# A two-block model on one core: the gates' product in column groups, the decay rows as split halves, SiLU moved to the second job

## The chip, the cores and the metric

The kernel runs on one core of a Trainium2 chip. The time is the device time of one execution in microseconds (us). Five engines work side by side and meet at semaphores: PE (TensorE, matrix products), DVE (VectorE), ACT (ScalarE), POOL (GpSimd) and SP (SyncE, which issues most DMAs).

## The reference

Two blocks run one after the other over 256 positions of width 1024. The change lies in the first layer of the first block, a gated delta rule with 8 heads, cut here to what matters:

```python
qkv = jax.nn.silu(causal_conv(proj[..., :3072], w_conv))        # q, k, v
a = proj[..., 4096:4104]; b = proj[..., 4104:4112]              # 16 more columns: the gates
g = -jnp.exp(a_log) * jax.nn.softplus(a + dt_bias)              # 8 heads x 256 positions
beta = jax.nn.sigmoid(b)
g = jnp.cumsum(g, axis=-1)                                      # within a chunk
decay = jnp.exp(jnp.where(tril, g[..., :, None] - g[..., None, :], -jnp.inf))
a_mat = jnp.where(strict, einsum(k * beta, k) * decay, 0.0)     # solved against
```

Behind it come the rest of this layer, an attention layer, and a second block whose conditioning vector also passes a SiLU (`cond = silu(c)`). These are not touched but for the place of that one SiLU and of one Square.

## The kernel before

**Jobs.** All large projections are cut into 104 jobs of 256 output columns. A chunk of weights (1 MB) comes by DMA into one of three slots `raw`. ACT rounds each half of it into `whi` (helper `high`, L1013), DVE subtracts to get the remainder `wlo` (helper `low`, L1444), and PE multiplies three times per tile (`whi` by `hhi`, `whi` by `hlo`, `wlo` by `hhi`; all at L489, 48 products a job, 8 tiles k of 6 products). Products of these split halves (type fp32r in the profile) stand in for one exact float32 product. Job J accumulates in bank `ps0` or `ps1` in turn.

**Jobs 0 to 7** make keys and queries, two heads a job. Each is followed by a convolution of four taps: the first tap on ACT (`first_tap`, L1092), three on DVE (`conv(J)`, L1511, 6 instructions), then SiLU on ACT (`silu(J)`, L1097). After an odd job PE sums the squares of the keys (`key_sums`), which waits for a Square of ACT (L1102). The loop of DVE is, for each J, `low(J + 1)` and then `conv(J)`; that of ACT is `high(J + 1)`, `silu(J - 1)`, `first_tap(J)`. The order on each engine is the order in which the code is written.

**The gates.** Behind job 0 PE multiplies the 16 gate columns (`w_ab`, held in the arena) by the unsplit activations `hf_a` in 8 float32 products that accumulate in `ps3[0:16]`, then one small product for attention biases (`onehot`). DVE makes the gate rows `rt16` from it behind `conv(0)` (L1560, L1562), ACT takes their Exp and Ln in job 1, DVE scans them behind `conv(2)` into `r16` (row h: summed log decay of head h).

**The delta rule.** Behind job 7, `decay_rows(p)` spreads the rows of two heads over 128 partitions: for each head one float32 product of `r16[:, 0, :]` (16 partitions x 256) by a column of the identity. ACT reads the bank (`state_decay`, L1141), PE adds the causal mask (`masked(p)`), ACT takes the Exp (`decay`, L1150), DVE multiplies (`pair_matrices`). Pieces of job 8 (`parts(8, ...)`) stand between. Then triangular inverses are built level by level (`lv` 1 to 6), each level with a job (9 + lv) beside it. Job 11 writes over the bank that `conv(9)` reads, so PE waits for `conv(9)` before it; on DVE this stands behind the scaling of keys (L1652), `low(11)` and `take_rows(1)` (L1629).

**POOL** sets constants at the start and, once `conv(0)` is done, builds masks and identity copies, last a copy of 128x2048 numbers (L426). PE starts when six of the first memsets are counted (`ones_ok`).

## Time and profile before

| | us |
|---|---|
| median of 3 runs | 833.12 (832.19 to 843.05) |
| the profiled execution, its own time | 833.37 |
| span of its profile | 831.5 |
| PE busy | 814.4 (98%) |
| DVE busy | 603.0 (73%) |
| ACT busy | 486.6 (59%) |
| POOL busy | 43.6 (5%) |

The profiled execution took 1.9 us more than its span, and 0.25 us more than the median. A row of the timeline gives the start, the time, engine and line, what is written and read, the number of instructions merged into it, and in brackets how long the engine had been idle and what released it. A float32 product is recorded as two instructions. Ends of products are modelled and overlap; the distance of their starts is the better measure.

### The profile page before, as it was taken

The page shows a single profiled execution, that of the slowest core. Times are in us where ns is not written, and L with a number is a line of the kernel's source. Part 1 is how long each engine was busy: PE and PEld are TensorE (multiplying, and loading weights), DVE is VectorE, ACT ScalarE, POOL GpSimd, SP SyncE. Part 2 cuts the span into 40 slices and gives each one's busy share as a digit, 9 for nine tenths or more (in the row PEclk, how much of TensorE's full clock was granted, in tenths as well). Part 3 has the DMA queues.
Part 4 walks back from the last instruction along what each step waited for, and adds up shares of the span by engine and source line. Part 5 has one row for each costly group of instructions (what it writes and reads, how often), then busy time and mean ns, then how long its engine had stood idle before and what let it go on. Part 6 is the DMA issues. An engine that isn't in the chain of part 4 may idle for free.

```text
span 831.5 us, 17292 instructions
## 1 busy us (share of the span) xinstructions
PE 814.4 (98%) x7278; PEld 793.7 (95%) x7278; DVE 603.0 (73%) x1049; ACT 486.6 (59%) x761; POOL 43.6 (5%) x68
## 2 busy tenths in 40 slices
PE   8999999999999999999999999989999999999998
PEld 7899999989999999999999999989999999999998
DVE  4776976678887876878797985556777867565662
ACT  5756756646855466553535354347777767677731
POOL 0500000018000100000000001000000000000000
PEclk9999999999999999999999999999999999999999
DMA  7363234526866884386666664973555644443450
GB/s 289 113 240 110 103 108 149 148 82 218 252 227 236 224 328 153 109 296 208 248 208 248 222 236 127 247 232 107 203 199 203 207 149 153 152 166 140 152 178 26
DMA packets 26493, 153.78 MB, mean 185 GB/s; under 512 B 2848, under 2 KB 3376, under 8 KB 12080
## 3 DMA queue, kind: packets, MB, share of 16 engines
q1 hardware_dynamic: 24432, 146.37, 50.3%
q0 software_dynamic: 1984, 6.31, 4.0%
q8 instruction: 58, 0.95, 0.5%
q14 instruction: 19, 0.16, 0.1%
HBM read 150.04 MB, written 2.62 MB: 184 GB/s over the span
## 4 chain that ended last, share of the span: by engine, by line
PE 84%; DVE 7%; DMA 4%; ACT 3%; issue 1%; SPq 0%; DVEq 0%; ACTq 0%
PE ps L489 83%; DMA raw<-weights 4%; DVE wlo L1444 3%; ACT whi L1013 1%; PE ps L869 1%; DVE early L1629 0%; DVE hlo L1472 0%; DVE arena L1476 0%; DVE early L1511 0%; DVE arena L1511 0%; DVE arena L1652 0%; DVE ada_ring L1525 0%; DVE olo L1489 0%; ACT hhi L1043 0%; PE ps L738 0%
## 5 line engine op out<-in xcount | busy, mean ns | idle before, releaser
L1444 DVE TENSOR_TENSOR wlo<-raw,whi 128x1024 fp32r<-128x1024 f32 x224 | 267.7, 1232 | 113.8 <-ACT whi L1013 113.8
L489 PE MATMUL ps<-hhi,whi 128*128 128x256 f32 x1024 | 295.0, 288 | 5.3 <-DVE hlo L1472 1.7
L489 PE MATMUL ps<-hlo,whi 128*128 128x256 f32 x1024 | 290.2, 283 | 0.0
L489 PE MATMUL ps<-hhi,wlo 128*128 128x256 f32 x1024 | 290.1, 283 | 0.0
L1013 ACT ACTIVATE whi<-raw 128x1024 fp32r<-128x1024 f32 x224 | 227.1, 1054 | 88.2 <-PE ps L489 60.9
L489 PEld LDWEIGHTS ps<-hhi,whi 128*128 128x128 f32 x1024 | 196.5, 192 | 8.2 <-issue 5.3
L489 PEld LDWEIGHTS ps<-hlo,whi 128*128 128x128 f32 x1024 | 196.7, 192 | 0.4
L489 PEld LDWEIGHTS ps<-hhi,wlo 128*128 128x128 f32 x1024 | 196.6, 192 | 0.0
L489 PE MATMUL ps<-ohi,whi 128*128 128x256 f32 x448 | 128.8, 287 | 1.4 <-DVE olo L1489 1.3
L489 PE MATMUL ps<-olo,whi 128*128 128x256 f32 x448 | 126.7, 283 | 0.0
L489 PE MATMUL ps<-ohi,wlo 128*128 128x256 f32 x448 | 126.7, 283 | 0.0
L489 PEld LDWEIGHTS ps<-ohi,whi 128*128 128x128 f32 x448 | 85.9, 192 | 2.8 <-issue 2.1
L489 PEld LDWEIGHTS ps<-olo,whi 128*128 128x128 f32 x448 | 85.9, 192 | 0.5 <-issue 0.5
L489 PEld LDWEIGHTS ps<-ohi,wlo 128*128 128x128 f32 x448 | 85.9, 192 | 0.0
L489 PE MATMUL ps<-arena 128*128 128x256 f32 (+2 forms) x496 | 76.5, 303 | 1.1 <-DVE olo L1489 1.1
L489 PEld LDWEIGHTS ps<-arena 128*128 128x128 f32 (+1 forms) x496 | 69.0, 187 | 7.4 <-issue 3.2
L489 PE MATMUL ps<-whi,hhi 128*128 128x256 f32 x256 | 72.6, 284 | 0.0
L489 PE MATMUL ps<-whi,hlo 128*128 128x256 f32 x256 | 72.4, 283 | 0.0
L489 PE MATMUL ps<-wlo,hhi 128*128 128x256 f32 x256 | 72.4, 283 | 0.0
L1525 DVE SCALAR_TENSOR_TENSOR ada_ring<-ada_ring,sil 128x256 f32<-128x256 f32 x144 | 59.0, 478 | 0.0
L489 PEld LDWEIGHTS ps<-whi,hhi 128*128 128x128 f32 x256 | 49.0, 192 | 0.7 <-issue 0.4
L489 PEld LDWEIGHTS ps<-whi,hlo 128*128 128x128 f32 x256 | 49.1, 192 | 0.3
(232 smaller groups left out, 961.4 us busy)
## 6 DMA issues: line engine op xcount, KB each, us to landing
raw<-weights SPq DMA_DIRECT2D x112, 1024.0 KB, 5.0
ada_ring<-ada SPq DMA_DIRECT2D x24, 1024.0 KB, 5.1
arena<-bias_rows_d POOLq DMA_DIRECT2D x4, 512.0 KB, 15.8
x<-x_t SPq DMA_DIRECT2D x2, 512.0 KB, 4.7
arena<-bias_rows_b POOLq DMA_DIRECT2D x4, 256.0 KB, 7.8
bias_rows_d<-turns POOLq DMA_DIRECT2D x1, 1024.0 KB, 13.3
arena<-bias_rows_d POOLq DMA_DIRECT2D x4, 256.0 KB, 19.5
out_t<-x SPq DMA_DIRECT2D x4, 256.0 KB, 2.4
```

The lines of the kernel that those rows point to most:

```text
L489: return pe.matmul(o, l, r, start=start, stop=stop, skip_group_check=skip)
L869: m = pe.transpose(turned_bank(hh, soft0)[:, a * P:a * P + P], ts[:, hh, c0:c0 + P], ident)
L1013: act.activation(whi[:, unit % UNITS, :, :], raw[:, c % RAW, 4 * half:4 * half + 4, :], ACT.Copy).then_inc(hi_ok_sem, 1)
L1444: dve.tensor_tensor(wlo[:, unit % UNITS, :, :], raw[:, c % RAW, 4 * half:4 * half + 4, :], whi[:, unit % UNITS, :, :].bitcast(F32), ALU.su ...
L1525: own(dve.scalar_tensor_tensor(out=b, in0=b, scalar=sil[:, k:k + 1], in1=ring[:, :, k - 2, :], op0=ALU.mult, op1=ALU.add))
```

## The change

Three things are changed.

1. *The gates' product.* The 8 products of the gate columns go to four groups of 32 output partitions of `ps6`, group k mod 4, two to a group. The first four read 32 columns, of which the upper 16 belong to the next tile and are ignored later. DVE copies the bank to `ab_quarters` (in the arena) ahead of `conv(0)`. In the midst of job 1, at tile 4, PE adds up the four groups with one float32 product by `ab_join`, a matrix of zeros and ones that DVE reduces from the identity. The gate rows are then made in turn J = 1, ahead of `conv(1)`.
2. *The decay rows.* Behind `conv(3)` DVE rounds `r16[:, 0, :]` into `r48[0:16]` (fp32r) and subtracts to get `rlo`; a DMA on POOL's queue moves `rlo` to `r48[32:48]`; the rest of `r48` is set to zero by a seventh memset at the start. `decay_rows` multiplies `r48` (48 partitions) by a column of `pick48`, which has a one at h and at 32 + h: one fp32r product a head instead of one float32 product.
3. *SiLU.* The Square of `final_norm` and the SiLU of `cond`, both 128x8, leave ACT's stretch between the activations' split and `high(1)`, and stand behind `first_tap(1)`. The SiLU's table load moves with it, to the front of `silu(0)`.

```diff
@@ pool
             pool.memset(rt16[:, 3, :], 1.0).then_inc(ones_ok_sem, 1)
+            pool.memset(r48[:, :].bitcast(F32), 0.0).then_inc(ones_ok_sem, 1)
             pool.wait_ge(conv_ok_sem, 1)
...
+            pool.wait_ge(rows_lo_sem, 1)
+            pool.dma_start(r48[32:48, :], rlo[:, :]).then_inc(rows_up_sem, 16)
             pool.wait_ge(bias_sb_sem, 1)
@@ tensor
+            def ab_rows():
+
+                pe.wait_ge(ab_copy_sem, 2)
+                mm(ps[3][0:16, 0:S], ab_join[:, :], ab_quarters, True, True).then_inc(ab_ok_sem, 1)
...
                     for k in range(KT):
-                        m = mm(ps[3][0:16, 0:S], A(6144, 8, 16)[:, k, :], hf_a[:, k, :], k == 0, k == KT - 1)
-                    m.then_inc(ab_ok_sem, 1)
+                        g, rows = k % 4, 32 if k < 4 else 16
+                        m = mm(ps[6][32 * g:32 * g + rows, 0:S], A(6144 + 16 * k, rows), hf_a[:, k, :], k < 4, True)
+                    m.then_inc(ab_quarter_sem, 1)
...
-                job(2 * i + 1, "T", hhi, hlo)
+                job(2 * i + 1, "T", hhi, hlo, at={4: ab_rows} if i == 0 else {})
...
-                    m = mm(ps[2 + 3 * (p % 2)][:, hh * S:hh * S + S], ident[0:16, h:h + 1].to_broadcast([16, P]), r16[:, 0, :], hh == 0, False)
+                    m = mm(ps[2 + 3 * (p % 2)][:, hh * S:hh * S + S], pick48[:, h:h + 1].to_broadcast([48, P]), r48[:, :], hh == 0, False)
...
+            pe.wait_ge(rows_up_sem, 16)
+            pe.wait_ge(rows_lo_sem, 2)
             decay_rows(0)
@@ scalar
             split_h(0, hf_a, hhi)
-            act.activation(gq, cols[:, COLS["final_norm"]:COLS["final_norm"] + KT], ACT.Square).then_inc(gq_ok_sem, 1)
             act.wait_ge(cols_in_sem, 16)
-            act.activation(sil[:, :], cols[:, COLS["cond"]:COLS["cond"] + KT], ACT.Silu).then_inc(sil_ok_sem, 1)
...
                 first_tap(J)
                 if J == 1:
 
+                    act.activation(gq, cols[:, COLS["final_norm"]:COLS["final_norm"] + KT], ACT.Square).then_inc(gq_ok_sem, 1)
+                    act.activation(sil[:, :], cols[:, COLS["cond"]:COLS["cond"] + KT], ACT.Silu).then_inc(sil_ok_sem, 1)
                     ln_exp_set()
@@ vector
+            dve.wait_ge(const_in_sem, 16)
+            dve.tensor_reduce(ab_join[:, :], ident.rearrange("p (g a) -> p a g", g=4)[:, 0:16, :], AX.X, ALU.add).then_inc(ab_copy_sem, 1)
             for J in range(8):
                 low(J + 1)
-                conv(J)
                 if J == 0:
+                    dve.wait_ge(ab_quarter_sem, 1)
+                    dve.tensor_copy(ab_quarters, ps[6][:, 0:S]).then_inc(ab_copy_sem, 1)
+                if J == 1:
                     dve.wait_ge(ab_ok_sem, 1)
...
+                conv(J)
+                if J == 0:
                     dve.wait_ge(bias_ps_sem, 1)
...
+                if J == 3:
+                    dve.wait_ge(rows_ok_sem, 2)
+                    own(dve.tensor_copy(r48[0:16, :], r16[:, 0, :]))
+                    dve.wait_ge(dve_own_sem, steps[0])
+                    dve.tensor_tensor(rlo[:, :], r16[:, 0, :], r48[0:16, :].bitcast(F32), ALU.subtract).then_inc(rows_lo_sem, 1)
+                    dve.tensor_tensor(pick48[:, :], ident[0:48, 0:16], ident[0:48, 32:48], ALU.add).then_inc(rows_lo_sem, 1)
```

On PE, between job 0 (bank `ps0`) and job 1 (`ps1`), before:

```order
L489 MATMUL ps0<-hhi,wlo 128x256
L489 MATMUL ps3<-early,arena 16x256 [waits ab_in]
L489 MATMUL ps3<-early,arena 16x256 x7
L489 MATMUL ps4<-cst,arena 8x256 [waits rel_in]
L489 MATMUL ps1<-hhi,whi 128x256 [waits lo_ok,conv_ok]
```

and in the changed kernel, where the last rows are those in the midst of job 1:

```order
L503 MATMUL ps0<-hhi,wlo 128x256
L503 MATMUL ps6<-early,arena 32x256 [waits ab_in]
L503 MATMUL ps6<-early,arena 32x256 x3
L503 MATMUL ps6<-early,arena 16x256 x4
L503 MATMUL ps4<-cst,arena 8x256 [waits rel_in]
L503 MATMUL ps1<-hhi,whi 128x256 [waits lo_ok,conv_ok]
...
L503 MATMUL ps1<-hhi,wlo 128x256
L503 MATMUL ps3<-arena,ab_join 16x256 [waits ab_copy,lo_ok]
L503 MATMUL ps1<-hhi,whi 128x256
```

The gates' product goes to bank `ps6` in eight pieces with the join behind tile 3 of job 1, where PE now waits for DVE's copy.

On DVE, from the last split of the activations to the three taps of `conv(1)`, before (`ps0` is read by `conv(0)`, `ps1` by `conv(1)`):

```order
L1470 TENSOR_TENSOR hlo<-early,hhi 128x256 [waits hh_ok] x2
L1444 TENSOR_TENSOR wlo<-raw,whi 128x1024 [waits hi_ok,ones_ok]
L1444 TENSOR_TENSOR wlo<-raw,whi 128x1024 [waits hi_ok]
L1511 SCALAR_TENSOR_TENSOR arena<-ps0,columns,arena 128x255 [waits tap_ok]
...
L1511 SCALAR_TENSOR_TENSOR arena<-ps0,columns,arena 128x254 [waits dve_own] x2
...
L1560 TENSOR_SCALAR arena<-ps3,columns 16x256 [waits ab_ok]
L1562 SCALAR_TENSOR_TENSOR arena<-arena 16x256 [waits dve_own]
L1564 COPY early<-ps4 8x256 [waits bias_ps]
L1444 TENSOR_TENSOR wlo<-raw,whi 128x1024 [waits hi_ok] x2
L1511 SCALAR_TENSOR_TENSOR arena<-ps1,columns,arena 128x255 [waits tap_ok]
```

and in the changed kernel:

```order
L1492 TENSOR_TENSOR hlo<-early,hhi 128x256 [waits hh_ok] x2
L1578 TENSOR_REDUCE ab_join<-cst 128x16 [waits const_in,ones_ok]
L1466 TENSOR_TENSOR wlo<-raw,whi 128x1024 [waits hi_ok] x2
L1583 COPY arena<-ps6 128x256 [waits ab_quarter]
L1533 SCALAR_TENSOR_TENSOR arena<-ps0,columns,arena 128x255 [waits tap_ok]
...
L1533 SCALAR_TENSOR_TENSOR arena<-ps0,columns,arena 128x254 [waits dve_own] x2
...
L1592 COPY early<-ps4 8x256 [waits bias_ps]
L1466 TENSOR_TENSOR wlo<-raw,whi 128x1024 [waits hi_ok] x2
L1586 TENSOR_SCALAR arena<-ps3,columns 16x256 [waits ab_ok]
L1588 SCALAR_TENSOR_TENSOR arena<-arena 16x256 [waits dve_own]
L1533 SCALAR_TENSOR_TENSOR arena<-ps1,columns,arena 128x255 [waits tap_ok]
```

The copy of `ps6` now stands ahead of `conv(0)`, and the two gate instructions (16x256) have moved from behind `conv(0)` to behind `low(2)`.

On ACT, from the activations' split to the block of `ln_exp_set`, before:

```order
L1041 ACTIVATE hhi<-early 128x256 [waits hf_ok] x8
L1075 ACTIVATE gq<-columns 128x8
L1077 ACT_TABLE_LOAD
L1077 ACTIVATE sil<-columns 128x8 [waits cols_in]
L1013 ACTIVATE whi<-raw 128x1024 [waits lo_ok,w_units,raw_in1] x2
...
L1092 ACTIVATE arena<-ps,columns 128x256
...
L1097 ACTIVATE arena<-arena 128x512 [waits conv_ok]
L1102 ACTIVATE early<-arena 128x512 [waits ss_col,silu_ok]
L1092 ACTIVATE arena<-ps,columns 128x256 [waits w_units]
...
L1002 ACT_TABLE_LOAD
L1116 ACTIVATE arena<-arena 16x256 [waits rows_ok,gq_ok]
```

and in the changed kernel:

```order
L1063 ACTIVATE hhi<-early 128x256 [waits hf_ok] x8
L1035 ACTIVATE whi<-raw 128x1024 [waits w_units,lo_ok,raw_in1,cols_in]
L1035 ACTIVATE whi<-raw 128x1024 [waits lo_ok,w_units,raw_in1]
...
L1035 ACTIVATE whi<-raw 128x1024 [waits lo_ok,w_units,raw_in2] x2
L1117 ACT_TABLE_LOAD
L1117 ACTIVATE arena<-arena 128x512 [waits conv_ok]
L1122 ACTIVATE early<-arena 128x512 [waits ss_col,silu_ok]
L1112 ACTIVATE arena<-ps,columns 128x256 [waits w_units]
...
L1134 ACTIVATE sil<-columns 128x8
L1024 ACT_TABLE_LOAD
L1138 ACTIVATE arena<-arena 16x256 [waits rows_ok,gq_ok]
```

The table load and the SiLU of 128x8 have left the place ahead of `high(1)`; the load stands ahead of `silu(0)`.

## Rows read from the trace of the kernel before

**Rows 1.** The page's busy times: engine, us (share) xinstructions.

```profile
PE 814.4 (98%) x7278; PEld 793.7 (95%) x7278; DVE 603.0 (73%) x1049; ACT 486.6 (59%) x761; POOL 43.6 (5%) x68
```

**Rows 2.** The timeline, 19 to 25 us: start us, us, engine, line, [idle before <-releaser].

```profile
19.24 0.19 ACT L1075 ACTIVATE gq<-columns 128x8 f32<-128x8 f32 x1
...
19.45 1.28 ACT L1077 ACT_TABLE_LOAD   x1
...
20.86 1.99 ACT L1013 ACTIVATE whi<-raw 128x1024 fp32r<-128x1024 f32 x2
...
20.93 3.63 PE L489 MATMUL ps<-early,arena 128*16 128x256 f32 x16
22.00 2.36 DVE L1444 TENSOR_TENSOR wlo<-raw,whi 128x1024 fp32r<-128x1024 f32 x2 [2.21 <-ACT whi L1013]
```

**Rows 3.** The timeline of PE, 102 to 104 us: products in tiles of 32x32.

```profile
102.55 1.26 PE L489 MATMUL ps<-early 32*32 32x16 f32 x128
103.74 0.38 PE L489 MATMUL ps<-hhi,whi 128*128 128x256 f32 x1
```

**Rows 4.** The timeline of ACT, DVE and POOL, 26 to 41 us.

```profile
26.73 0.63 ACT L1097 ACTIVATE arena<-arena 128x512 f32<-128x512 f32 x1 [1.27 <-DVE arena L1511]
...
31.06 0.84 ACT L1092 ACTIVATE arena<-ps,columns 128x256 f32<-128x256 f32 x2 [3.02 <-PE ps L489]
...
31.92 1.28 ACT L1002 ACT_TABLE_LOAD   x1
...
35.11 1.99 ACT L1013 ACTIVATE whi<-raw 128x1024 fp32r<-128x1024 f32 x2
...
36.19 1.23 DVE L1444 TENSOR_TENSOR wlo<-raw,whi 128x1024 fp32r<-128x1024 f32 x1 [1.82 <-ACT whi L1013]
...
36.85 2.31 POOL L426 COPY arena<-cst 128x2048 f32<-128x2048 f32 x1
...
37.33 2.92 DVE L1444 TENSOR_TENSOR wlo<-raw,whi 128x1024 fp32r<-128x1024 f32 x1
```

**Rows 5.** The timeline of PE, 30 to 46 us.

```profile
30.86 0.95 PE L489 MATMUL ps<-ones,early 128*128 128x1 f32 x8
...
43.96 1.05 PE L489 MATMUL ps<-ones,early 128*128 128x1 f32 x8 [0.42 <-ACT early L1102]
...
45.65 0.35 PE L489 MATMUL ps<-hhi,whi 128*128 128x256 f32 x1 [0.63 <-DVE wlo L1444]
```

**Rows 6.** Windows: stretch, its length, busy us (xinstructions) of each engine, PEclk, DMA share, GB/s.

```profile
40.00:50.00 10.00, 8.95 (x62) 8.69 (x61) 9.93 (x21) 6.18 (x9) 0.00 (x0) 0.83 0.53 182
...
48.00:49.00 1.00, 1.00 (x7) 1.00 (x7) 1.00 (x4) 0.00 (x0) 0.00 (x0) 0.50 0.74 246
...
80.00:100.00 20.00, 20.00 (x204) 18.69 (x204) 18.12 (x37) 14.26 (x33) 0.00 (x0) 1.00 0.17 58
```

**Rows 7.** The timeline of PE, 72 to 79 us.

```profile
72.53 1.99 PE L489 MATMUL ps<-r,cst 16*128 16x256 f32 x8
74.45 2.94 PE L489 MATMUL ps<-arena 128*128 128x128 f32 x24
...
77.36 0.28 PE L489 MATMUL ps<-hlo,whi 128*128 128x256 f32 x1
...
78.54 0.28 PE L489 MATMUL ps<-hhi,wlo 128*128 128x256 f32 x1
78.66 0.39 PE L489 MATMUL ps<-causal_r,ident_r 128*128 128x512 f32 x1
```

**Rows 8.** The timeline of ACT, DVE and PE, 77 to 110 us.

```profile
77.67 0.64 ACT L1141 ACTIVATE early<-ps 128x256 f32<-128x256 f32 x2
...
79.09 2.18 ACT L1150 ACTIVATE early<-ps,hc 128x128 f32<-128x128 f32 x8 [0.78 <-PE ps L489]
...
99.42 2.16 DVE L1652 TENSOR_SCALAR arena<-ps,ecol 128x128 f32<-128x128 f32 x8 [0.70 <-PE ps L728]
...
110.11 0.38 PE L489 MATMUL ps<-hhi,whi 128*128 128x256 f32 x1 [0.58 <-DVE early L1511]
```

More of the change, by code:

```diff
@@ L92, in two_blocks @@
         hlo = sb("hlo", [P, KT, S], F32R)
+        rows_ctx = ExitStack()
+        r48 = rows_ctx.enter_context(nc.sbuf_tensor("r48", [48, S], F32R))
+        rlo = rows_ctx.enter_context(nc.sbuf_tensor("rlo", [16, S], F32R))
+        rows_ctx.close()
         early_ctx = ExitStack()
@@ L190, in two_blocks @@
         rcol = sb("rcol", [16, 1])
+        ab_quarters = A(17408, S)
+        ab_join = sb("ab_join", [P, 16])
+        pick48 = sb("pick48", [48, 16], F32R)
         fd = turns[0:16, 0:2, :].rearrange("p a b -> p (a b)")
@@ L278, in two_blocks @@
         ab_ok_sem = sem("ab_ok")
+        ab_quarter_sem = sem("ab_quarter")
+        ab_copy_sem = sem("ab_copy")
+        rows_lo_sem = sem("rows_lo")
+        rows_up_sem = sem("rows_up")
         rows_ok_sem = sem("rows_ok")
@@ L403, in _ @@
             pool.memset(rt16[:, 3, :], 1.0).then_inc(ones_ok_sem, 1)
+            pool.memset(r48[:, :].bitcast(F32), 0.0).then_inc(ones_ok_sem, 1)
             pool.wait_ge(conv_ok_sem, 1)
             pool.wait_ge(lmask_in_sem, 16)
-            pool.wait_ge(ones_ok_sem, 6)
+            pool.wait_ge(ones_ok_sem, 7)
             pool.wait_ge(const_in_sem, 16)
@@ L567, in keep_warm @@
                     mm(ps[5][:, 0:P], ones[:, :], ones[:, :], True, True)
-            pe.wait_ge(ones_ok_sem, 6)
+            pe.wait_ge(ones_ok_sem, 7)
             keep_warm(20)
@@ L1070, in _ @@
                 act.activation(xsq_a[:, 2 * t:2 * t + 2, :], x[:, 2 * t:2 * t + 2, :], ACT.Square).then_inc(xsq_ok_sem, 1)
-            act.wait_ge(ones_ok_sem, 6)
+            act.wait_ge(ones_ok_sem, 7)
             high(0)
@@ L1552, in mod_of_slot @@
                 take_mod(n, b, free)
-            dve.wait_ge(ones_ok_sem, 6)
+            dve.wait_ge(ones_ok_sem, 7)
+            dve.wait_ge(const_in_sem, 16)
+            dve.tensor_reduce(ab_join[:, :], ident.rearrange("p (g a) -> p a g", g=4)[:, 0:16, :], AX.X, ALU.add).then_inc(ab_copy_sem, 1)
             for J in range(8):
                 low(J + 1)
-                conv(J)
                 if J == 0:
+                    dve.wait_ge(ab_quarter_sem, 1)
+                    dve.tensor_copy(ab_quarters, ps[6][:, 0:S]).then_inc(ab_copy_sem, 1)
+                if J == 1:
                     dve.wait_ge(ab_ok_sem, 1)
```

## The prediction

> **What bounds the kernel now.** I read the busy times first: PE is busy 98% of the span [rows 1], so time goes only if PE's own stream gets shorter, or one of its few waits does. The whole change lies in the first 110 us. So I read the timeline there engine by engine, from each wait of PE back to what released it, and then the windows for the granted clock. The reader is to see four things.
>
> First, the gates' product: 16 records, 8 products, in 3.63 us, 0.45 us each [rows 2]. Second, the chain that starts job 4. Job 1 ends at 30.86 [rows 5]; ACT has waited 3.02 us for that and starts the first tap at 31.06, loads a table at 31.92, works through the gates' Exp and Ln and comes to `high(3)` only at 35.11; DVE starts `low(3)` at 36.19 after 1.82 us of waiting [rows 4]. Its second half takes 2.92 us where the first took 1.23, while POOL's copy runs from 36.85 to 39.16. Two turns later PE waits 0.63 us for `low(4)` and starts job 4 at 45.65 [rows 5]. What PE does ahead of that, from job 3's end to 45.65, is little: 0.42 us of waiting, eight records of one column in 1.05 us, 0.63 us of waiting. Third, behind it the granted clock is 0.50, the lower level of 1.2 GHz, and 0.83 in the mean of 40 to 50 us [rows 6]: 17% of 10 us is 1.7 us of work lost. Fourth, PE waits 0.58 us for `conv(9)` at 110.11, on a chain in which DVE had waited 0.70 us for PE's transposes before 99.42 [rows 8].
>
> **The gates' product.** An unsplit product alone costs 0.45 us. How far products to four column groups overlap, no row of this trace shows at this width. The nearest is the level products in tiles of 32x32: 128 records, 64 products of 16 columns, from 102.55 to 103.74, 18.6 ns a product [rows 3]. By 0.45 us for 256 columns, 16 columns cost 28 ns, so these overlap 1.5 times at least, and changing the tile from product to product costs no drain. A product is two records in a row to the same group, and the second must follow the first; if starts keep the order of the code, the next group can begin only beside the second record. That gives one product per 0.23 us, 28/2 = 14 ns for 16 columns, near the 18.6 of the row. I take this: 7 x 0.23 + 0.45 = 2.0 us, a saving of 1.6. Ends: overlap of all four groups, 0.9 us (saving 2.7), since fp32r products take 256 columns each 0.118 us (ten of them between 77.36 and 78.54 [rows 7]), so feeding columns at that pace is possible; and none, 3.6.
>
> The Trainium skill, page "TensorEngine Tiling (Array Packing)", gives up to 4x for tiles of 32 columns (section "Theoretical Speedup") and says that tiles load and multiply in parallel (section "Key Properties"). By it the product would be the 0.9 us of the end above; the row at 16 columns shows 1.5, and no run here shows 4. The same section says that changing the tiling mode drains the engine, which speaks against the join: it stands in the midst of job 1 and changes the mode twice.
>
> The join is one more product of 0.45 us. What entering and leaving a narrower form costs I take from the first decay rows: four products from 72.53 to 74.45, 1.92 us, of which 4 x 0.45 = 1.80 are product [rows 7]; so 0.12, and the join is 0.6. PE's stream to the end of job 1 is then shorter by 1.6 - 0.6 = 1.0 (between -0.6 and 2.1).
>
> Does job 1's start find its weights? It would move from 25.0 (3.63 us and the small `onehot` product behind 20.93) to 23.4. Today the first half of `low(1)` ends near 23.2 (22.00 and half of 2.36) [rows 2]. ACT loses Square, table load and SiLU there, from 19.24 to 20.86, so `high(1)` and `low(1)` come 1.6 us earlier: ready at 21.6. At the end of 0.9 us, with a start at 22.3, the move of SiLU is what makes the gain possible; at 2.0 it hardly is. The copy of `ps6` on DVE, behind it `conv(0)`, `low(2)`: these have the time until the join, 2.9 us into job 1, so PE doesn't wait for the copy. The new reduction of 128x16 falls into DVE's 2.21 us of waiting [rows 2] and costs nothing; the seventh memset delays PE's warm-up products by 0.3 us at the start, and they end in a wait for ACT and DVE.
>
> **The moved SiLU.** Its table load of 1.28 us now stands ahead of `silu(0)`, where ACT waited 1.27 us for `conv(0)`, and 3.02 us more before the first tap of job 1 [rows 4]. It is hidden; without that cover it would be 1.3. Square and SiLU themselves, behind that tap, are on the chain: 19.24 to 19.45 and about as long again less overlap, 0.3 together. So `high(3)` comes 1.0 - 0.3 = 0.7 us earlier.
>
> **From there to job 4.** POOL starts at `conv(0)`, and its casts wait for `low(2)`, which comes some 1.7 us earlier (it no longer waits for ACT, and the gate instructions stand behind it). So POOL's copy is ready near 35.15, and `low(3)` near 35.5: the order may turn. If `low(3)` still comes first, everything moves by 0.7. If the copy comes first, `low(3)` waits up to 2 us, but both halves then follow at 1.2 each and end 0.4 to 0.9 us earlier than the 40.25 of today. Either way job 4 starts 0.4 to 0.7 us earlier; I take **0.7**. The clock's fall I take as it is now.
>
> The Trainium skill, page "SBUF — State Buffer", section "Who interferes with whom", says that a DVE instruction with two inputs in SBUF and a reading one of POOL exclude each other, and that the order of issue decides who waits. The 2.92 us agree with it. The rival on a hole ahead of job 3 is this rule at work.
>
> The three new DVE instructions behind `conv(3)` are narrower than half a `low` (1.2 us, [rows 4]) and sit ahead of `low(5)`, which PE needs only after job 4. The DMA of POOL then has until 72.53. Nothing else queues on POOL before the attention biases. Cost: nothing.
>
> **The decay rows.** Eight float32 products become eight fp32r products at 0.118 us. The first four take 1.92 us today and 4 x 0.12 + 0.12 = 0.6 afterwards, 1.3 less; the later two pairs 0.65 less each; 2.6 in all. But it does not all reach the end. `masked(0)` at 78.66 would be ready 1.3 us earlier, and must wait for the first half of `state_decay(0)`, done near 78.05 [rows 7, 8]. ACT and DVE gain 0.5 there. DVE then is busy 18.12 of the 20 us from 80 on [rows 6], so it keeps 0.5 while PE gains 1.8 in all. At 99.42 DVE's wait of 0.70 for PE goes too: 0.5 + 0.7 = **1.2**. PE's wait at 110.11 grows from 0.58 to 1.2 accordingly, and behind it PE carries on. At nearest bounds this term is 0.5 (the 0.70 goes to something else) to 1.8.
>
> **The sum.** 0.7 + 1.2 = 1.9 us off 833.37, or 831.5; the median of the runs stands 0.25 below the profiled execution, so **831.2**.
>
> **The rivals.**
> 1. *The clock doesn't fall behind job 3.* The quiet stretch shifts and is split otherwise. Next late would be what PE waits for at 110.11 [rows 8], and job 4 isn't tied to that. It gives back 1.7: 829.5. For it: the fall rests on one stretch. Against: that stretch is still there. Chance 0.25.
> 2. *All four groups overlap.* 1.1 us more: 830.1, and with rival 1 in addition 828.4. Chance 0.17 together.
> 3. *The groups don't overlap*, so that the change doesn't do what it says: 8 x 0.45 as before, plus join 0.6 and ACT 0.3, so -0.9 + 1.2: 832.8. Against it stand the 18.6 ns. Chance 0.12.
> 4. *A hole ahead of job 3, slower than before.* POOL's copy comes ahead of `low(3)`; job 2 ends near 36.5 (0.95 and 48 x 0.118 behind 30.86, less 1.0) and job 3 finds its weights only near 38.7. PE stands for 2 us and the clock falls there as well: job 3 takes 1.7 us longer, job 4 starts 1.5 us later than today, and falls again. -1.5 + 1.2 is 0.3 to 0.4 slower: 833.5. It decides if both falls happen; with only the first one the time is 831.8. Chance 0.10.
>
> **Chances and range.** The forecast itself, 831.2 give or take half a microsecond, has 0.36. Rivals 1 to 3 lie between 828.4 and 832.8, and runs of one kernel spread by some tenths; 828.5 to 833.2 takes them in but for about half of the doubled case of rival 2, and leaves out rival 4: 0.15 outside. A measurement of this kernel can tell about 2% (17 us) from no change, and none of the cases comes near it: faster 0.01, same 0.98, slower 0.01.
>
> **What the profile afterwards would show.** The 16 records to `ps6` in 2.0 us (0.9 or 3.6 for the rivals); job 1's end 1.0 us earlier than 30.86; `high(3)` near 34.4; whether POOL's copy starts before `low(3)`, and the longest of its halves; the granted clock between 36 and 50 us; decay rows of 0.6 us; `masked(0)` waiting for ACT; L1652's counterpart 1.2 us earlier against job 4's start, and a longer wait of PE for `conv(9)`. The prediction is wrong if job 4 doesn't start earlier, or if the clock falls in another place.

## The result

| | median us | lowest to highest | executions |
|---|---|---|---|
| before | 833.25 | 830.49 to 843.05 | 20 |
| changed | 828.55 | 824.65 to 838.96 | 20 |

The ratio is 0.9941, 95% interval 0.9928 to 0.9954: 4.7 us less, under the 2% that counts as a difference here, and two and a half times the forecast's 1.9. The time lies inside the range given, but by 0.05 us only (its lower end was 828.5); the likeliest case, 831.2, was wrong. Here and below medians take in all executions, and ratios leave out those more than 1.5% above the fastest of their kernel.

The profiled execution of the changed kernel, 838.96 us, is the slowest of its 20. Weights of a later part came late in it, DVE waited 8.05 us for them, and PE behind it 6.74; two rows of its timeline:

```profile
287.61 0.61 DVE L1544 TENSOR_SCALAR ada_ring<-ada_ring,sil 128x256 f32<-128x256 f32 x2 [8.05 <-DMA ada_ring<-ada]
295.13 1.11 PE L891 MATMUL ps<-cst,arena 128*128 128x128 f32 x4 [6.74 <-DVE arena L1805]
```

No edit is near that place, and the kernel before can have it too: the profile of e7, which is before with five products added, shows DVE waiting 7.00 us for the same DMA. On e7's chip (e5 to e8) 14 of 35 executions of the unchanged kernel took 838 to 846 us; that the late DMA is the reason there too is likely and not shown. The times of those four experiments are not used, only their first 110 us. So the changed kernel was profiled again (e1 below: 825.83 us, span 823.8); up to 270 us the two profiles agree within 0.3 us. All rows of the changed kernel from here to the experiments are from that second profile. The page's busy times, to set beside [rows 1]:

```profile
PE 807.2 (98%) x7272; PEld 788.4 (96%) x7272; DVE 604.4 (73%) x1054; ACT 486.3 (59%) x761; POOL 45.5 (6%) x70
```

PE is busy 7.2 us less, at the same 98%: the time came out of PE's own stream. Of this difference between two single profiles, 3.4 us are a slower clock in the profile of before (see the third step below). The timeline of PE, 20 to 30 us, answers to [rows 2] and the first of [rows 5]:

```profile
20.91 1.07 PE L503 MATMUL ps<-early,arena 128*32 128x256 f32 x16
21.91 0.59 PE L503 MATMUL ps<-cst,arena 32*8 32x256 f32 x2
22.43 0.39 PE L503 MATMUL ps<-hhi,whi 128*128 128x256 f32 x1
...
25.29 0.28 PE L503 MATMUL ps<-hhi,wlo 128*128 128x256 f32 x1
25.50 0.60 PE L503 MATMUL ps<-arena,ab_join 128*16 128x256 f32 x2
26.04 0.39 PE L503 MATMUL ps<-hhi,whi 128*128 128x256 f32 x1
26.26 0.28 PE L503 MATMUL ps<-hlo,whi 128*128 128x256 f32 x1
...
29.01 0.95 PE L503 MATMUL ps<-ones,early 128*128 128x1 f32 x8
```

Before, the small product behind the gates' product started here:

```profile
24.49 0.59 PE L489 MATMUL ps<-cst,arena 32*8 32x256 f32 x2
```

The 16 records to `ps6` take 1.07 us instead of 3.63; by starts 1.00 (20.91 to 21.91) instead of 3.56 (20.93 to 24.49). Two products of job 1 with the join between them start 0.97 us apart (25.29 to 26.26), where two steps of 0.12 would be usual: the join costs 0.73. Job 1 ends at 29.01 instead of 30.86. ACT, DVE and POOL behind it, beside [rows 4]:

```profile
29.21 0.84 ACT L1112 ACTIVATE arena<-ps,columns 128x256 f32<-128x256 f32 x2 [2.56 <-PE ps L503]
...
33.46 1.99 ACT L1035 ACTIVATE whi<-raw 128x1024 fp32r<-128x1024 f32 x2
...
34.53 4.05 DVE L1466 TENSOR_TENSOR wlo<-raw,whi 128x1024 fp32r<-128x1024 f32 x2 [2.02 <-ACT whi L1035]
...
35.28 2.23 POOL L438 COPY arena<-cst 128x2048 f32<-128x2048 f32 x1
```

`high(3)` begins at 33.46 (before 35.11), `low(3)` still comes ahead of POOL's copy, and its second half is still held: 4.05 us for two. Then PE up to job 4 and two windows (PE, PEld, DVE, ACT, POOL busy; PEclk is the number behind these five), beside [rows 5, 6]:

```profile
42.31 1.05 PE L503 MATMUL ps<-ones,early 128*128 128x1 f32 x8 [0.42 <-ACT early L1122]
43.99 0.36 PE L503 MATMUL ps<-hhi,whi 128*128 128x256 f32 x1 [0.63 <-DVE wlo L1466]
```

```profile
40.00:50.00 10.00, 8.95 (x74) 8.56 (x73) 9.90 (x21) 4.54 (x8) 0.64 (x1) 1.00 0.55 204
48.00:49.00 1.00, 1.00 (x11) 1.00 (x10) 1.00 (x2) 0.00 (x0) 0.64 (x1) 1.00 1.01 418
```

The same two waits of PE stand there, 1.66 us earlier, but the granted clock stays at 1.00, the upper level of 2.4 GHz, where before it was 0.50 and 0.83 in the mean. Last, the decay rows and what follows, beside [rows 7, 8]:

```profile
69.39 0.73 PE L503 MATMUL ps<-r,pick 48*128 48x256 f32 x4
70.05 2.94 PE L503 MATMUL ps<-arena 128*128 128x128 f32 x24
74.94 0.50 PE L503 MATMUL ps<-causal_r,ident_r 128*128 128x512 f32 x1 [0.52 <-ACT early L1163]
...
89.92 2.43 DVE L1533 SCALAR_TENSOR_TENSOR early<-ps,columns,early 128x255 f32<-128x255 f32 x6 [0.20 <-ACT early L1112]
...
94.55 1.64 DVE L1686 TENSOR_SCALAR arena<-ps,ecol 128x128 f32<-128x128 f32 x6
...
105.24 0.38 PE L503 MATMUL ps<-hhi,whi 128*128 128x256 f32 x1 [0.58 <-DVE early L1533]
```

Four decay rows take 0.66 us by starts (1.92 before), `masked(0)` now waits for ACT, DVE's scaling of keys (L1686) no longer waits for the transposes, and PE's wait for `conv(9)` has moved from 110.11 to 105.24. The next key sums behind job 4, before and now:

```profile
59.25 0.95 PE L489 MATMUL ps<-ones,early 128*128 128x1 f32 x8
```

```profile
56.11 0.95 PE L503 MATMUL ps<-ones,early 128*128 128x1 f32 x8
```

Of the 4.87 us at `conv(9)`, 1.66 were there at job 4's start; job 4 and what follows up to the next key sums took 12.12 us instead of 13.60, which is the clock's 1.48; 1.73 came between there and 105.24.

### The profile page after: what moved, and what is told of

Same layout as the page of the kernel before. It is cut to its first block, busy times and chain, and to the rows that moved or that the text cites. A ratio compares the mean times of both kernels' runs of the same rounds, so it can differ in the third digit from the quotient of the medians.

```text
span 837.0 us, 17290 instructions
## 1 busy us (share of the span) xinstructions
PE 811.7 (97%) x7272; PEld 792.2 (95%) x7272; DVE 604.2 (72%) x1054; ACT 486.4 (58%) x761; POOL 44.1 (5%) x70
## 4 chain that ended last, share of the span: by engine, by line
PE 79%; DVE 9%; DMA 6%; ACT 4%; issue 2%; SPq 0%; DVEq 0%; ACTq 0%
PE ps L503 78%; DMA raw<-weights 4%; DVE wlo L1466 3%; DMA ada_ring<-ada 2%; ACT whi L1035 1%; PE ps L891 1%; DVE ada_ring L1547 1%; DVE early L1533 1%; DVE arena L1533 1%; DVE early L1663 0%; DVE hlo L1494 0%; DVE arena L1498 0%; ACT L1024 0%; DVE arena L1686 0%; DVE olo L1511 0%
```

## The experiments

All times in one table; "before" ran beside each. The last three columns are of the one profile of each kernel: start of job 4, PE's wait for `conv(9)` (110.11 in the profile of before), and where in the first 80 us the granted clock fell. The times of e5 to e8 are given but not used (see above), and one execution of e12 took 3963 us and counts in its median only.

| kernel | median us (n) | ratio, 95% interval | job 4 | `conv(9)` | falls |
|---|---|---|---|---|---|
| e1 changed | 826.84 (5) | 0.9937, 0.9917 to 0.9957 | 43.99 | 105.24 | none |
| e2 without decay rows | 832.80 (12) | 0.9989, 0.9966 to 1.0012 | 44.06 | 111.74 | 44, 72 |
| e3 SiLU at its old place | 828.30 (9) | 0.9954, 0.9940 to 0.9969 | 44.30 | 107.03 | 44 |
| e4 groups in a row | 826.72 (5) | 0.9939, 0.9917 to 0.9960 | 44.04 | 105.29 | none |
| e5 SiLU alone | 837.52 (12) | 0.9974, 0.9920 to 1.0028 | 45.60 | 110.18 | 72 |
| e6 decay rows alone | 838.47 (12) | 1.0023, 0.9981 to 1.0066 | 45.55 | 108.28 | 44 |
| e7 before, filled | 844.15 (12) | 1.0092, 1.0054 to 1.0130 | 45.85 | 112.03 | 72 |
| e8 changed, filled | 837.73 (12) | 0.9986, 0.9937 to 1.0034 | 43.90 | 105.14 | none |
| e9 POOL's copy late | 826.73 (6) | 0.9915, 0.9899 to 0.9931 | 43.55 | 104.79 | none |
| e10 and the tap first | 825.89 (6) | 0.9910, 0.9892 to 0.9928 | 42.67 | 103.94 | none |
| e11 two groups | 828.25 (6) | 0.9939, 0.9924 to 0.9954 | 44.83 | 107.56 | 44 |
| e12 gates alone | 831.71 (12) | 0.9983, 0.9969 to 0.9997 | 44.21 | 108.79 | 72 |
| e13 before | 835.03 (1) | | 45.61 | 111.68 | 44, 72 |
| e14 changed | 826.90 (1) | | 44.12 | 105.36 | none |
| e15 gates alone | 831.04 (1) | | 44.27 | 108.88 | 72 |
| e16 as e3 | 827.12 (1) | | 44.19 | 105.42 | none |
| e17 decay rows thrice | 834.43 (11) | 0.9997, 0.9964 to 1.0029 | 43.96 | 106.80 | 44 |
| e18 changed | 829.21 (5) | 0.9946, 0.9925 to 0.9968 | 43.98 | 105.23 | none |

**e1, e14, e18: the changed kernel.** 

> The changed kernel once more, for a profile and for its scatter. Theory A (the gain is PE's shorter stream and the shorter chain to job 4, and a clock fall behind job 3 that is gone because the quiet stretch moved): time 828.5 +/- 0.7, job 4 starts near 43.9 us and takes 5.9 to 6.0 us at a granted clock of 1.00. Rival B (the clock's fall behind job 3 comes and goes from run to run whatever the kernel): the same start of job 4, but in this profile job 4 may take 7.5 us as in the kernel before, and the runs fall in two heaps 1.7 us apart.

It has 826.84 and no fall, with the rows above; two more profiles, below, agree to 0.2 us. The times of the changed kernel scatter around the forecasts made for them: 826.84 is below theory A's 827.8, and e18's 829.21 above its 828.

**e4: do the groups need an order?**

```diff
-                        g, rows = k % 4, 32 if k < 4 else 16
-                        m = mm(ps[6][32 * g:32 * g + rows, 0:S], A(6144 + 16 * k, rows), hf_a[:, k, :], k < 4, True)
+                        g, rows = k // 2, 16 if k % 2 else 32
+                        m = mm(ps[6][32 * g:32 * g + rows, 0:S], A(6144 + 16 * k, rows), hf_a[:, k, :], k % 2 == 0, True)
```

> The changed kernel with the two products of a column group one behind the other (group k // 2 instead of k mod 4); the same sums. Theory A (a product that must wait for its own group holds back those behind it, so overlap needs neighbours in different groups): the eight products take 2 to 3 us instead of 1.07, job 4 starts 1 to 1.9 us later, 829.5 to 830.5. Rival B (each group has its own order and the code's order is nothing): 1.07 us as before and 828.5.

The code now gives the two products of a group one behind the other. The timeline of PE, once from its start and once from 21.39 on; 128*32 are the first products of the four groups, 128*16 the second ones, and they alternate in the code:

```profile
20.94 0.66 PE L503 MATMUL ps<-early,arena 128*32 128x256 f32 x8
...
21.39 0.64 PE L503 MATMUL ps<-early,arena 128*16 128x256 f32 x8
```

All eight records of the first kind start before any of the second. So PE started the products in another order than the code's; the rows fit a product that waits for its own group alone. The whole takes 1.09 us by records and 1.02 by starts, the same as in e1 (1.07 and 1.00). The step of the prediction "if starts keep the order of the code" is refuted here.

**e11: two groups.**

```diff
-                        g, rows = k % 4, 32 if k < 4 else 16
-                        m = mm(ps[6][32 * g:32 * g + rows, 0:S], A(6144 + 16 * k, rows), hf_a[:, k, :], k < 4, True)
+                        g, rows = k % 2, 32 if k < 2 else 16
+                        m = mm(ps[6][32 * g:32 * g + rows, 0:S], A(6144 + 16 * k, rows), hf_a[:, k, :], k < 2, True)
```

DVE's copy and the join take 64 rows instead of 128.

> The changed kernel with the gates' product in two column groups (k mod 2) instead of four; the join then takes 64 rows. An unsplit product costs 0.45 us, eight in four groups took 1.07 us together. Theory A (each group is as slow as one product alone and groups run beside each other without limits): eight products in two groups take 4 x 0.45 = 1.8 us, and job 4 starts up to 0.7 us later than at 43.9. Rival B (the gain comes from something else than the groups, such as that a narrow product costs less than 0.45 whatever its group): near 1.07 us. Rival C (two of the four groups share a path, so that two groups that don't share it already give all): near 1.07 us as well; the 3.63 us of one group stands against rival B alone.

```profile
20.91 1.92 PE L503 MATMUL ps<-early,arena 128*32 128x256 f32 x16
22.76 0.59 PE L503 MATMUL ps<-cst,arena 32*8 32x256 f32 x2
```

Four products deep it takes 1.92 us (by starts 1.85), two deep 1.00, eight deep 3.56: about 0.45 for each product in the longest group, and at most 0.1 once. Theory A holds, B and C don't, and job 4 starts 0.84 later than in the changed kernel. The times can't tell a difference of 0.8 between kernels that ran on different chips, and here the clock fell at job 4 besides.

**e3, e5, e12: what the moved SiLU is worth.** e3 is the changed kernel with Square and SiLU ahead of `high(1)` again; e5 is before with only these moved; e12 is before with only the gates' part.

```diff
             split_h(0, hf_a, hhi)
+            act.activation(gq, cols[:, COLS["final_norm"]:COLS["final_norm"] + KT], ACT.Square).then_inc(gq_ok_sem, 1)
             act.wait_ge(cols_in_sem, 16)
+            act.activation(sil[:, :], cols[:, COLS["cond"]:COLS["cond"] + KT], ACT.Silu).then_inc(sil_ok_sem, 1)
...
-                    act.activation(gq, cols[:, COLS["final_norm"]:COLS["final_norm"] + KT], ACT.Square).then_inc(gq_ok_sem, 1)
-                    act.activation(sil[:, :], cols[:, COLS["cond"]:COLS["cond"] + KT], ACT.Silu).then_inc(sil_ok_sem, 1)
```

> The changed kernel with Square, SiLU and its table load back ahead of high(1) on ACT. Theory A: job 1 starts at 23.1 instead of 22.3, high(3) comes 0.5 us later (0.8 less the 0.3 of Square and SiLU), but POOL's copy now comes 2 us later and lets both halves of low(3) through at 1.2 us each, so job 4 starts 0.1 to 0.5 us later: 829.0. Rival B: the whole 1.6 us that ACT got back reaches job 4: 830.2.

> The kernel before with the third part of the change alone: Square and SiLU behind the first tap of job 1. The gates' product keeps its 3.63 us. Theory A: low(1) comes 1.6 us earlier but job 1's start stays at 25.0, bound by PE; the chain behind gets 0.3 us longer: no change to 0.3 us slower, 833.3 to 833.6. Rival B: ACT's 1.6 us are worth something by themselves: 832 or less.

> The kernel before with the gates' product in column groups and its join, but decay rows as float32 products and SiLU and Square at their old place. Theory A (the parts add up): the start is like that of the changed kernel with SiLU at the head, job 4 at 44.3, 1.35 us earlier than before; decay rows take 1.92 us and `conv(9)` is waited for 1.4 to 1.7 us earlier than before (108.4 to 108.7) where the clock doesn't fall; the time is 1.4 to 1.7 below that of the kernel before. Rival B (the gates' part alone gains only with SiLU out of the way, since `low(1)` is late): job 1 starts no earlier than 23.4 and job 4 no earlier than 45.2. Observation to be tested besides: every kernel with float32 decay rows behind an earlier job 4 has shown a fall of the granted clock at 72 to 79; it should show one here, worth up to 1.5 us, and then the time is within 0.5 of the kernel before.

In e12 PE reaches job 1 before its weights:

```profile
21.87 0.59 PE L493 MATMUL ps<-cst,arena 32*8 32x256 f32 x2
23.24 0.36 PE L493 MATMUL ps<-hhi,whi 128*128 128x256 f32 x1 [0.77 <-DVE wlo L1454]
```

and job 1 ends at 29.78, in e3 at 29.87, against 29.01. Yet job 4 starts only 0.2 to 0.3 later, since POOL's copy, now at 37.9, no longer holds `low(3)` (2.78 us for two). Alone (e5) the move gives 0.05 at job 4. Both parts are needed for the 1.85 at job 1's end, but the move of SiLU adds only 0.2 to 0.3 of the 0.8 there to job 4's start. The rest goes because, with SiLU moved, POOL's copy holds `low(3)` again (4.05 us for two).

**e2, e6: the decay rows.** e2 is the changed kernel with float32 decay rows, e6 is before with the split halves only.

```diff
-                    m = mm(ps[2 + 3 * (p % 2)][:, hh * S:hh * S + S], pick48[:, h:h + 1].to_broadcast([48, P]), r48[:, :], hh == 0, False)
+                    m = mm(ps[2 + 3 * (p % 2)][:, hh * S:hh * S + S], ident[0:16, h:h + 1].to_broadcast([16, P]), r16[:, 0, :], hh == 0, False)
```

> The changed kernel with the decay rows as they were (float32 products of 16 partitions; no r48, no DMA on POOL's queue). Theory A (what the decay rows gained is 0.6 us at masked(0) and 1.1 us at the transposes behind job 9): nothing changes up to job 4, the time rises by 1.7 to 830.2. Rival B (their gain is swallowed by DVE's chain and the gain there came with the earlier jobs): under 0.5 us, 829.0. Rival C (the whole of PE's 2.6 us counts): 831.1.

> The kernel before with the decay rows as split halves alone. Theory A: masked(0) 0.6 us earlier against job 7's end and the counterpart of L1652 1.7 us earlier: 831.5. Rival B (the two gains need each other): 833.

PE's wait for `conv(9)` in e6:

```profile
108.28 0.44 PE L499 MATMUL ps<-hhi,whi 128*128 128x256 f32 x1 [0.58 <-DVE early L1523]
```

e6 and the profile of before have the same fall at job 4 (13.59 and 13.60 us from its start to the next key sums), so they can be compared directly: `conv(9)` at 108.28 against 110.11, of which 0.10 is there at job 4's start. The decay rows alone give **1.7**.

In e2 all three theories are too low: its median is 6.0 us above that of the changed kernel on the same chip (832.80 against 826.84) and no better than before (0.9989, interval across 1), though job 4 starts as early as in e1. Two falls lie in its profile:

```profile
44.00:48.00 4.00, 3.94 (x22) 3.97 (x23) 4.00 (x8) 1.52 (x3) 0.00 (x0) 0.63 0.39 137
72.00:76.00 4.00, 4.00 (x17) 3.27 (x16) 1.72 (x6) 2.33 (x5) 0.00 (x0) 0.54 0.52 217
76.00:80.00 4.00, 4.00 (x24) 4.00 (x23) 0.46 (x2) 0.73 (x4) 0.00 (x0) 0.60 0.00 0
```

The two windows from 72 on lose 4 x 0.46 + 4 x 0.40 = 3.4 us of clock, twice what this part gains. Seven of e2's twelve executions have a mean clock of 0.993 or 0.994, which only one of e1's five has. So the times of the parts don't simply add up.

**e7, e8: filling PE's quiet stretch.** Two products of 128x128 before and three behind the key sums of job 3, in before and in the changed kernel.

```diff
+                if i == 1:
+                    keep_warm(2)
                 key_sums(i)
+                if i == 1:
+                    keep_warm(3)
```

> The kernel before with five more products of ones that nobody reads: two between job 3 and the key sums, three between these and job 4, into a bank that is idle. They leave the data alone and fill PE's two waits (0.42 and 0.63 us). Theory A (the clock falls because of the quiet stretch ahead of job 4): the granted clock stays at 1.00 in 40 to 52 us, job 4 takes 5.9 us and the time falls by 1.2 to 1.7: 831.8. Rival B (the fall has nothing to do with the stretch): job 4 takes 7.5 us as before and the time stays within 0.3.

> The changed kernel with the same five products. Theory A (with the change the fall is gone anyway): no gain, 828.5 +/- 0.5. Rival B (the fall comes and goes in the changed kernel too, and its median holds some of it): 0.5 to 1.5 us faster, 827.5.

In e7 the fall at job 4 is missing, but one at 72 has come. The filling costs nothing that shows: job 4 starts 0.20 later than before, but the gates' product does so already (21.13 against 20.93). By e5, which has no filling and no fall at job 4 either, the absence proves nothing. Inconclusive. All twelve executions of e7 took 841.9 us or more, where 14 of 35 of before took 838 or more; whether the filling has a part in that is open.

**e13 to e16: whose is a fall?** The same kernels profiled again.

> The kernel before, once more. Theory K (a fall of the granted clock belongs to the kernel): falls again at 46.5 to 49.9 and at 550 to 557, job 4 takes 7.4 us. Theory R (it belongs to the run): in this profile at least one of the two is missing or elsewhere; job 4 takes 5.9 us where it is missing.

> The changed kernel, a third profile. Theory K: no fall at job 4 or at 70 to 80, as in the two before it; job 4 from 43.9 to 49.9, `conv(9)` waited for at 105.2. Theory R: a fall may appear at job 4, which then ends near 51.4.

> The kernel with the gates' part alone, once more. Theory K: no fall at job 4 (44.2 to 50.1), one at 71 to 75 behind the float32 decay rows, `conv(9)` waited for at 108.8. Theory R: either may differ.

> The changed kernel with SiLU and Square at their old place, once more. Theory K: a fall at job 4 again (44.3 to 51.7). Theory R: it may be missing, job 4 then ends near 50.2, and `conv(9)` is waited for near 105.5 instead of 107.0.

The window from 44 to 48 of e3, and of e16, which is the same kernel:

```profile
44.00:48.00 4.00, 3.70 (x18) 3.73 (x19) 3.97 (x10) 1.66 (x3) 0.00 (x0) 0.57 0.39 109
```

```profile
44.00:48.00 4.00, 3.81 (x32) 3.84 (x33) 3.97 (x10) 1.66 (x3) 0.00 (x0) 1.00 0.42 133
```

The fall at job 4 belongs to the run, not to the kernel alone. It moves `conv(9)` from 105.42 to 107.03; 0.11 of this is there at job 4's start, so it costs 1.5. e13 has a fall at 72 that the first profile of before lacks (1.57 more at `conv(9)`), and lacks the one at 550. e14 and e15 repeat the pattern of e1 and e12, which fits both theories. A single case of the same kernel with and without is enough for theory R, and there is one at job 4, at 72 and at 550.

Whether the change makes a fall at job 4 rarer is open: three of five profiles without the gates' part have it (before, e6, e13), and four of 15 with it (e2, e3, e11, e17). A further place is right behind the wait for `conv(9)`, between 104 and 116 us: eight of the 20 profiles have a fall there (e5, e6, e10 to e13, e15, e18), with either form of the decay rows. One is in the changed kernel, e18:

```profile
104.00:108.00 4.00, 3.42 (x21) 3.18 (x18) 3.45 (x6) 3.82 (x10) 0.00 (x0) 0.62 0.02 10
```

The fall at 72 is not spread evenly. Of seven profiles with float32 decay rows, six have it (e2, e5, e7, e12, e13, e15; not the first of before); of 13 with the split halves, none.

**e17: is it the length of the narrow stretch?**

```diff
-                for hh in range(2):
+                for hh in [0, 1] * (3 if p < 2 else 1):
```

> The changed kernel, in which the first two pairs of decay rows are multiplied three times over (the same values): twelve fp32r products of 48 rows instead of four. They take 12 x 0.12 + 0.1 = 1.5 to 1.6 us instead of 0.66, near the 1.92 us of the four float32 products before. Theory L (a long stretch of narrow products is followed by the fall): the granted clock falls between 70 and 78, `conv(9)` is waited for at 107.5 to 108, and the time is 1.5 to 2.5 us above the changed kernel's. Theory F (only the float32 form, or its 1.92 us, does it): no fall; everything behind moves by 0.9, less what `masked(0)` waits for ACT anyway (0.52): `conv(9)` at 105.6 to 106.1, and the time 0.4 to 0.9 above the changed kernel's.

> The changed kernel beside the one above: 826 to 828 us, ratio 0.992 to 0.995, no fall at job 4 nor at 70 to 80, `conv(9)` at 105.2.

```profile
70.84 1.64 PE L503 MATMUL ps<-r,pick 48*128 48x256 f32 x12
```

```profile
70.00:74.00 4.00, 4.00 (x36) 3.86 (x35) 2.43 (x6) 1.34 (x3) 0.00 (x0) 1.00 0.67 248
```

Twelve products take 1.57 us by starts, and the clock stays at 1.00 there: for theory F, as far as one profile goes. But F's delay did not come. `conv(9)` is waited for at 106.80, 1.56 later than in e1, and 1.47 of this is the fall at 44; so eight products more, 0.9 us of PE, cost 0.1 there, where F had 0.4 to 0.9. `masked(0)`, which in e1 waits 0.52 for ACT, starts only 0.23 later against job 7's end. Its fall at 44 comes ahead of the edit, in instructions that are those of the changed kernel, which shows once more that a fall there is the run's. The times don't settle it: 827.0 to 829.4 in five executions, 834.4 to 837.2 in six, a gap that neither theory has, and the profile is of the first group. A late DMA as in the first profile of the changed kernel would make a gap of this size, but no profile of the second group exists; what makes it is open, and so is why the float32 rows bring the fall.

**e9, e10: beyond the change.** e9 makes POOL's copy wait for `low(3)`; e10 also takes the first tap of `conv(2)` ahead of `silu(1)`.

```diff
+            pool.wait_ge(lo_ok_sem, 8)
             pool.tensor_copy(tt[:, :, :], ident.unsqueeze(1).to_broadcast([P, 16, P])).then_inc(tt_ok_sem, 1)
@@ scalar, e10 only
+                if J == 2:
+                    first_tap(J)
                 if J:
                     silu(J - 1)
...
-                first_tap(J)
+                if J != 2:
+                    first_tap(J)
```

> The changed kernel, in which POOL waits for the eighth half of `wlo` (both halves of `low(3)` done) before its copy of 128x2048 numbers. In the changed kernel that copy runs from 35.19 to 37.42 and holds the second half of `low(3)`, so that two halves take 4.06 us instead of some 2.4. Theory A (the chain to job 4 goes on to DVE's `conv(2)` and then `low(4)`, but `conv(2)` also waits for ACT's first tap near 38.0): the two halves take 2.4 us, `conv(2)` starts at 38.0 instead of 38.4, job 4 starts 0.4 us earlier, at 43.5 to 43.6. Rival B (the hold is on the chain in full): job 4 starts 1.5 us earlier, at 42.3 to 42.4. Rival C (the copy, now later, collides with a tap or with `low(4)` instead): no gain, job 4 at 43.9 or later. Time: 0.4, 1.5 or 0 below the changed kernel when the granted clock doesn't fall.

> As the kernel with POOL's copy late, and ACT takes the first tap of `conv(2)` ahead of `silu(1)`. Theory A: neither ACT's tap nor POOL's copy holds `conv(2)`; it starts near 36.9, and job 4 near 42.5, 1.4 us ahead of the changed kernel's 43.9; the time is then about 1.4 us below that of the changed kernel, near 825.3, if the granted clock doesn't fall in it. Rival B (something else becomes late: `high(4)` behind ACT's longer stretch, or the load of its chunk of weights): job 4 starts at 43.5 or later, and the time is that of the changed kernel. Rival C: `key_sums` waits longer for ACT's Square of `silu(1)`, which is behind the tap now, and job 2 or 3 starts later; then there would be a wait of PE above 0.6 us there.

DVE in e9, and DVE and PE in e10:

```profile
34.43 2.36 DVE L1467 TENSOR_TENSOR wlo<-raw,whi 128x1024 fp32r<-128x1024 f32 x2 [2.02 <-ACT whi L1036]
38.05 2.43 DVE L1534 SCALAR_TENSOR_TENSOR arena<-ps,columns,arena 128x255 f32<-128x255 f32 x6 [1.26 <-ACT arena L1113]
```

```profile
36.78 2.42 DVE L1537 SCALAR_TENSOR_TENSOR arena<-ps,columns,arena 128x255 f32<-128x255 f32 x6
```

```profile
41.75 1.05 PE L504 MATMUL ps<-ones,early 128*128 128x1 f32 x8
42.67 0.36 PE L504 MATMUL ps<-hhi,whi 128*128 128x256 f32 x1
```

In e9 `low(3)` is 1.7 us shorter and `conv(2)` then stands 1.26 for the tap: 0.44 is left, as theory A had it. In e10 the tap is there, both waits of PE before job 4 are gone, job 4 starts 1.32 earlier than in e1, and `conv(9)` comes at 103.94, 1.30 earlier. Its 825.89 is the lowest median here, 0.8 below e9 on the same chip; the intervals of the two overlap, so the times don't tell them apart, and the 0.85 at `conv(9)` has to stand for it.

## Why the prediction was wrong

**What was right.** That the places where the change acts lie in the first 110 us, that PE's stream sets the time, that job 1's start would find its weights only with SiLU moved, that PE doesn't wait for the copy of `ps6`, that `low(3)` still comes first if job 1's end moves by one or two us, the 0.66 for four decay rows against 0.6, `masked(0)` held by ACT (0.5 forecast; its start moved 0.58 against the end of job 4), and DVE's 0.70 of waiting for the transposes, which is gone.

**The step that failed first: "7 x 0.23 + 0.45 = 2.0 us" for the gates' product.** It took 1.00 by starts. I had the product at its end of "overlap of all four groups, 0.9" and chose the middle, by 16-column products in a tile form of their own and an assumed order of starts; e4 shows that the order isn't kept. From there the sum runs: saving 2.56 instead of 1.6; join 0.73 instead of 0.6 (0.28 beside the 0.45, where the first decay rows had given 0.12 for the change of form); job 1's end 1.85 earlier instead of 1.0; Square and SiLU on the chain 0.2 instead of 0.3 (from job 1's end to `high(3)` 4.45 against 4.25), so `high(3)` 1.65 earlier; job 4 **1.66 instead of 0.7**. e11 and e12 fit the same sum with other sizes.

The Trainium skill, page "TensorEngine Tiling (Array Packing)", section "Theoretical Speedup", has up to 4x; 3.56 to 1.00 is 3.6, so the trace agrees. The Trainium skill, page "TensorE: Matmul & The Clock Gate", section "Part 3: Packing small matmuls — row/col tiling", says that products start and end in the order of the program. The rows of e4 differ from it for products to other column groups, and the measurement decides.

**The second: 1.2 for the decay rows; e6 shows 1.7.** The forecast followed DVE from `masked(0)` to 99.42 and called it bound between, since it was busy 18.12 of 20 us. But a wait was in that stretch, before:

```profile
94.03 2.43 DVE L1511 SCALAR_TENSOR_TENSOR early<-ps,columns,early 128x255 f32<-128x255 f32 x6 [0.48 <-ACT early L1092]
```

DVE stood 0.48 for ACT's first tap of `conv(9)`, and 0.20 now. Of the 0.5 that is missing, 0.28 are this. The other 0.22 is at the third pair: before, 2.48 us passed from the start of a `low` to the next instruction of `pair_matrices` (83.14 to 85.62), in e6 2.26 (82.57 to 84.83). PE's wait for `conv(9)` was to grow to 1.2 and stayed at 0.58 in every profile: the products of the level ahead of it start 3.2 us before it in before and in e1 alike (106.91 and 102.03), so they moved along with it.

**The third: "The clock's fall I take as it is now."** Rival 1 had its absence at 0.25, but both took a fall for a property of the kernel. e3 and e16 show that it comes and goes, at 1.5 us. So the profile of before, with two falls (46 to 50, 550 to 557), and that of e1, with none, differ by 7.7 us in span, 3.4 of them clock. How much of the medians' 4.7 is clock can be estimated from the executions, each with its mean granted clock. Of 53 of before (beside e1 to e4, e9 to e12, e17 and e18) and 31 of the changed kernel (the first 20, e1, e14, e18) I set those of equal clock side by side: at 0.998 medians of 831.6 (15) and 827.9 (9), at 0.996 832.9 (13) and 829.1 (6), 3.6 and 3.7 apart. The medians of all are 832.8 and 828.3, 4.5 apart: so **some 0.8** is clock. The estimate is loose: the same sum on executions drawn again at random from these gives 0 to 1.7 in 95% of draws. The changed kernel falls less often (half of its executions have 0.998 or more, a third of before's), which fits the rows at 72.

**The account.** Job 4's start 1.66, decay rows 1.7, clock 0.8: 4.2 of 4.7. The first two are shown by profiles, the third is an estimate, and that they add up in time is argued: e2, which lacks only the decay rows, is 6.0 us above the changed kernel beside it, not 1.7. The rest, 0.3 to 0.5, is not located. It doesn't have to be a part of its own: from the wait for `conv(9)` to PE's next wait for DVE, at 169 to 178 us, with instructions that are the same, the changed kernel takes 63.9, 64.1 and 64.4 us in e14, e1 and its first profile, and before 64.7. (e18 takes 65.0 and e13 66.3, both with a fall of the clock on the way.)

Put in the prediction's cases: it was rival 2 together with half of rival 1, which stood at 828.4 and "with rival 1 in addition", a small part of 0.17. That 828.4 is so near to the measured 828.55 is in part luck: its 1.7 for the clock is too much by 0.9, and its 1.2 for the decay rows too little by 0.5.

## What to carry to other kernels

When a stage is free to move along PE's stream, work out the whole chain for both ends of an unknown cost before choosing: here the end, not the middle, was right, and the gain reached job 4 almost whole. Follow the engine that a gain must pass through wait by wait; a share of busy time of 91% hid a wait of 0.48. And take a fall of the clock in a single profile for a draw, not for a cost: set executions side by side that have the same mean clock, or profile the same kernel again.

## What the runs showed of the hardware

- Float32 products to different column groups of 32 run side by side: 8 products of 128 rows by 256 columns in 3.56, 1.85 and 1.00 us in one, two and four groups (before, e11, e1). They start out of the code's order (e4).
- One such product of 16 columns between full-width ones costs 0.73 us of PE's stream, not its own 0.45 (e1).
- Falls of the granted clock to 0.50 at one place come and go between executions of one kernel, for 1.5 to 1.6 us in the first 110 us (e3 and e16, before and e13); the one at 72 in e2 lasted longer and took 3.4. Six of seven profiles with 1.92 us of float32 products of 16 rows behind key sums show one right behind them, and none of 13 with 0.66 to 1.6 us of fp32r products of 48 rows; the cause is open.
- A POOL copy of 128x2048 took 1.90 us with no `low` beside it and 2.21 to 2.76 with one; the half of `low` beside it took 2.9 us instead of 1.2 (before, e1, e11, e12, e17).
